# Inverting the 64x64 blocks of a delta-rule recurrence: recursion on compact 32x32 diagonal blocks instead of full-width 64x64 ones

## The reference

```
sa = einsum('bhij,bhj->bhi', s, kk_t)
s  = s * w_t[:, :, None, :] - sa[..., None] * b_t[:, :, None, :] + v_t[..., None] * k_t[:, :, None, :]
y  = einsum('bhij,bhj->bhi', s, r_t)
```

## Time and profile before

| | |
|---|---|
| median of 3 runs | 3817.77 us (3813.36 to 3818.82) |
| profiled execution | 3811.94 us, its span 3810.2 us |
| TensorE busy (matmuls) | 3230.0 us, 85% of the span |
| VectorE, ScalarE, GpSimd busy | 1983.3, 1128.4, 1046.2 us |
| the 12 passes of the recurrence | from about 2440 to 3098 us of the span |

### The profile page before, as it was taken

The page is one execution under the profiler, slowest core; times in us unless marked ns, Lnnn a source line. Parts: engine busy times, 40 slices in busy tenths (PEclk is TensorE's granted clock), DMA queues, the critical chain, the costliest instruction groups (busy, mean ns, idle before and its releaser), DMA issues. The chain is left out here.

```text
span 3810.2 us, 66276 instructions
## 1 busy us (share of the span) xinstructions
PE 3230.0 (85%) x28285; PEld 2544.4 (67%) x28285; DVE 1983.3 (52%) x2750; ACT 1128.4 (30%) x1783; POOL 1046.2 (27%) x608
## 2 busy tenths in 40 slices
PE   4989788999698879899945998599999987489896
PEld 2866476878486547687822887388888875369634
DVE  3766556880376665787022660466666633421152
ACT  2223334331322333433123221233333321322212
POOL 0321133544132213354400221243444411022100
PEclk7998899999898889999966999799999997789998
DMA  2221122333222102233334331200000021021101
GB/s 72 73 78 39 29 84 66 94 93 97 57 68 72 45 26 86 72 95 92 97 108 177 105 114 53 80 16 20 20 20 20 3 80 45 1 92 57 50 0 66
DMA packets 354104, 243.93 MB, mean 64 GB/s; under 512 B 22212, under 2 KB 330872, under 8 KB 353164
## 3 DMA queue, kind: packets, MB, share of 16 engines
q1 hardware_dynamic: 350398, 231.57, 20.3%
q10 hardware_dynamic: 3406, 8.04, 0.5%
HBM read 222.54 MB, written 17.04 MB: 63 GB/s over the span
## 5 line engine op out<-in xcount | busy, mean ns | idle before, releaser
L571 POOL TENSOR_TENSOR weights_lo<-weights_raw,weights_hi 128x1024 fp32r<-128x1024 f32 (+1 forms) x234 | 596.7, 2551 | 1227.8 <-ACT weights_hi L540 1227.8
L1139 PE MATMUL psum<-moving_hi,weights_hi 128*128 128x512 f32 x1488 | 604.2, 406 | 101.6 <-DVE weights_lo L571 53.8
L1139 PE MATMUL psum<-moving_lo,weights_hi 128*128 128x512 f32 x1488 | 590.2, 397 | 0.0
L1139 PE MATMUL psum<-moving_hi,weights_lo 128*128 128x512 f32 x1488 | 588.9, 396 | 0.0
L1139 PEld LDWEIGHTS psum<-moving_hi,weights_hi 128*128 128x128 f32 x1488 | 286.8, 193 | 184.2 <-DVE weights_lo L571 55.4
L540 ACT ACTIVATE weights_hi<-weights_raw 128x1024 fp32r<-128x1024 f32 (+2 forms) x250 | 253.9, 1019 | 291.0 <-PE psum L1139 240.3
L1139 PEld LDWEIGHTS psum<-moving_lo,weights_hi 128*128 128x128 f32 x1488 | 286.6, 193 | 61.9 <-issue 4.9
L1139 PEld LDWEIGHTS psum<-moving_hi,weights_lo 128*128 128x128 f32 x1488 | 286.1, 192 | 62.0
L1139 PE MATMUL psum<-hn_hi,even_hi 128*128 128x256 f32 (+1 forms) x480 | 162.9, 339 | 34.0 <-DVE even_lo L571 34.0
L2406 POOL TENSOR_TENSOR second_off<-second_mats,second_masks 128x256 f32<-128x256 f32 x180 | 141.3, 787 | 183.4 <-PE psum L1851 183.4
L571 POOL TENSOR_TENSOR even_lo<-even_raw,even_hi 128x1024 fp32r<-128x1024 f32 x28 | 67.5, 2409 | 361.1 <-ACT even_hi L540 361.1
(11 more groups left out here) (430 smaller groups left out, 6959.9 us busy)
## 6 DMA issues: line engine op xcount, KB each, us to landing
weights_raw<-in_w_up SPq DMA_DIRECT2D x88, 512.0 KB, 3.9
weights_raw<-in_w_in SPq DMA_DIRECT2D x78, 512.0 KB, 3.8
ada_raw<-in_ada_w SPq DMA_DIRECT2D x12, 2048.0 KB, 18.5
odd_raw<-in_od_w_in SPq DMA_DIRECT2D x16, 1024.0 KB, 5.4
even_raw<-in_ev_w_in SPq DMA_DIRECT2D x30, 512.0 KB, 3.9
weights_raw<-in_w_down SPq DMA_DIRECT2D x32, 448.0 KB, 3.7
weights_raw<-in_w_o SPq DMA_DIRECT2D x16, 512.0 KB, 4.1
weights_raw<-in_w_down SPq DMA_DIRECT2D x16, 512.0 KB, 4.1
```

The source lines that it names most:

```text
L571: ops.tensor_tensor(self.ring.lo[i % n][:, a:b], self.ring.raw[:, t % self.ring.landing, a:b], self.ring.hi[i % n][:, a:b].bitcast(F32), A ...
L1139: return nc.tensor.matmul(to, (hi, lo)[which][:, at:at + P], moving(k)[part], start=start and k == 0 and i == 0, stop=stop and k == n_k - ...
```

## The change

M, y, W and the mask `off` of the first four levels are kept *compactly*: only the two 32x32 diagonal blocks of each 64x64 matrix, one in 32 partitions, the other in the 32 below. So a chunk's matrix is 128 partitions by 32 columns, and a 64x64 product of two halves becomes four 32x32 products on the four diagonal tiles of the array, at rows and columns 0, 32, 64 and 96:

```
+def quarters_matmul(nc, out, lhsT, rhs):
+    for j in range(4):
+        ps = slice(HB * j, HB * j + HB)
+        last = nc.tensor.matmul(out[ps, :], lhsT[ps, :], rhs[ps, :], start=True, stop=True)
+    return last
+
+def halves_of_chunks(nc, out, lhsT, rhs):
+    for j in range(4):
+        hf, at = slice(64 * (j // 2), 64 * (j // 2) + 64), slice(HB * (j % 2), HB * (j % 2) + HB)
+        last = nc.tensor.matmul(out[HB * j:HB * j + HB, :], lhsT[hf, at], rhs[hf, at], start=True, stop=True)
+    return last
```

The unit "m" becomes "blocks": the diagonal blocks of M transposed and of M, both from PSUM. VectorE masks both at once into `wc` (the compact W, columns 0 to 31 transposed, 32 to 63 not), and ScalarE copies M transposed to `mt`, from which `off` is cut:

```
-                                last = halves_matmul(nc, to[:, c, :], ar[:, x, a_], bk[:, x, a_])
+                                halves_of_chunks(nc, to[:, c, 0:HB], bk[:, x, a_], ar[:, x, a_])
+                                last = halves_of_chunks(nc, to[:, c, HB:], ar[:, x, a_], bk[:, x, a_])
...
+                    pe.wait_ge(blocks_copied, GROUPS)
...
+                        elif what == "blocks":
+                            act.wait_ge(taken_dve, taken_by(n, "dve"))
+                            S.activation(mt[:, own(g), :], bank(n % BANKS, CH)[:, :, 0:HB], ACT.Identity).then_inc(blocks_copied, 1)
...
-                                made = V.tensor_tensor(buf.wb[:, slots(g), CH:], bank(n % BANKS, CH), over(pre_f + "1"), ALU.mult)
+                                made = V.tensor_tensor(wc[:, own(g), :], bank(n % BANKS, CH), over(pre_t + "1"), ALU.mult)
```

The rounds. Levels 0 to 3 (blocks 2 to 16) use `quarters_matmul`; the last level (block 32) needs one 32x32 product for y and one for W in each head and chunk, and its result isn't added but copied into its corner of `wb`:

```
                             for c in range(4):
-                                last = halves_matmul(nc, bank_y(n)[:, c, :], off[:, n % 2, c, :], buf.wb[:, slots(g).start + c, CH:])
+                                if level < last_level:
+                                    last = quarters_matmul(nc, bank_y(n)[:, c, :], off[:, n % 2, c, :], wc[:, x, HB:])
+                                else:
+                                    for hf in range(2):
+                                        last = PE.matmul(bank_y(n)[half(hf, other), c, :], buf.mats[half(hf, first), slots(g).start + c, columns_of(other)],
+                                                         wc[half(hf, first), x, HB:], start=True, stop=True)
...
                             for c in range(4):
-                                last = halves_matmul(nc, bank_w(n)[:, c, 0:CH], y_, wt)
                                 if level < last_level:
-                                    last = halves_matmul(nc, bank_w(n)[:, c, CH:], wt, y_)
+                                    quarters_matmul(nc, bank_w(n)[:, c, 0:HB], y_, wt)
+                                    last = quarters_matmul(nc, bank_w(n)[:, c, HB:], wt, y_)
+                                else:
+                                    for hf in range(2):
+                                        last = PE.matmul(bank_w(n)[half(hf, first), c, 0:HB], y_[half(hf, other), :], wt[half(hf, other), :],
+                                                         start=True, stop=True)
```

VectorE and GpSimd. The add shrinks to 128x256 elements; the last level has two copies of 32 partitions a group. GpSimd begins W with one addition of the identity where it had three operations, cuts `off` from `mt` (128x128 elements) and only for 12 rounds, and in place of the last three masks it writes the compact W into `wb` at full width (`widen`, two operations a group, zeros off the diagonal):

```
-                            n_cols = 2 * CH if level < last_level else CH
-                            w_ = buf.wb[:, slots(g), 0:n_cols]
-                            V.tensor_tensor(w_, w_, bank_w(n)[:, :, 0:n_cols], ALU.add).then_inc(w_added, 1)
+                            if level < last_level:
+                                w_ = wc[:, own(g), :]
+                                V.tensor_tensor(w_, w_, bank_w(n), ALU.add).then_inc(w_added, 1)
+                            else:
+                                dve.wait_ge(widened, 2 * g + 2)
+                                for hf in range(2):
+                                    V.tensor_copy(buf.wb[half(hf, first), slots(g), columns_of(other)], bank_w(n)[half(hf, first), :, 0:HB])\
+                                        .then_inc(last_copied, 1)
...
+                    def widen(g):
+                        pool.wait_ge(w_added, GROUPS * (last_level - 1) + g + 1)
+                        for j in range(2):
+                            G.tensor_scalar(buf.wb[:, slots(g), columns_of(j)], wc[:, own(g), 0:HB], mask("block")[:, j:j + 1], None, ALU.mult)\
+                                .then_inc(widened, 1)
```

More of the change, by code:

```diff
@@ L41 @@
 NCH = T2 // CH
+HB = CH // 2
 RET_HEADS = 8
@@ L108, in const_table @@
     t["eye64"] = s == q
-    for b in (1, 2, 4, 8, 16, 32):
+    s, q = p[:, None] % 32, np.arange(32)[None, :]
+    t["eye32"] = np.concatenate([s == q, s == q], 1)
+    for b in (1, 2, 4, 8, 16):
         off = (s // (2 * b) == q // (2 * b)) * (s // b != q // b)
-        t[f"up{b}"] = off * (s < q)
-        t[f"lo{b}"] = off * (s > q)
+        up, lo = off * (s < q), off * (s > q)
+        t[f"up{b}"] = np.concatenate([up, lo], 1) if b == 1 else up
+        t[f"lo{b}"] = np.concatenate([lo, up], 1) if b == 1 else lo
+    t["block"] = (p[:, None] // 32 % 2 == np.arange(2)[None, :]).astype(float)
     k64 = np.arange(64)
@@ L1933, in pe @@
             for c in range(4):
-                last = halves_matmul(nc, self.made(item, 2 * CH)[:, c, :], b.wb[:, s0 + c, 0:CH], b.ax[:, s0 + c, :])
+                last = halves_matmul(nc, self.made(item, 2 * CH)[:, c, :], b.wb[:, s0 + c, :], b.ax[:, s0 + c, :])
             last.then_inc(self.wau_ready, 1)
@@ L2253, in products @@
             pair_mask = "upper" if d == 0 else "lower"
-            pre_t, pre_f = ("up", "lo") if d == 0 else ("lo", "up")
+            pre_t = "up" if d == 0 else "lo"
+            first, other = (0, 1) if d == 0 else (1, 0)
+            half = lambda hf, j: slice(64 * hf + HB * j, 64 * hf + HB * j + HB)
+            columns_of = lambda j: slice(HB * j, HB * j + HB)
             over = lambda name: mask(name).unsqueeze(1).to_broadcast([P, 4, mask(name).shape[1]])
             bank = lambda b, n: psum[:, b * 512:b * 512 + 4 * n].rearrange("p (c n) -> p c n", n=n)
-            kinds = (["v"] if d == 0 else []) + ["tok", "kr", "br", "a", "m"]
+            kinds = (["v"] if d == 0 else []) + ["tok", "kr", "br", "a", "blocks"]
             units = [(g, what) for g in range(GROUPS) for what in kinds]
@@ L2270, in products @@
             BANKS = 4
-            bank_y, bank_w = lambda n: bank(n % 2, CH), lambda n: bank(2 + n % 2, 2 * CH)
-            names = "unit_ready taken_act taken_dve wt_scaled wt_begun wf_begun masked y_ready y_taken w_ready w_added "
+            bank_y, bank_w = lambda n: bank(n % 2, HB), lambda n: bank(2 + n % 2, CH)
+            names = "unit_ready taken_act taken_dve blocks_copied w_begun widened masked y_ready y_taken w_ready w_added last_copied "
             with stage(nc, names + Terms.NAMES + Recurrence.NAMES) as (block, sems):
[L2274 to L2277, removed]
+                (unit_ready, taken_act, taken_dve, blocks_copied, w_begun, widened, masked, y_ready, y_taken, w_ready,
+                 w_added, last_copied) = sems[:12]
+                terms = Terms(sems[12:12 + Terms.COUNT], i + 1, p - 1 if d == 1 and p else None)
+                rec = Recurrence(nc, sems[12 + Terms.COUNT:], i - 1, buf, psum, eye)
                 @block.sync
@@ L2293, in _ @@
                             pe.wait_ge(taken_act if by[n - BANKS] == "act" else taken_dve, taken_by(n - BANKS, by[n - BANKS]))
+                            if units[n - BANKS][1] == "blocks":
+                                pe.wait_ge(blocks_copied, units[n - BANKS][0] + 1)
                         to = bank(n % BANKS, width[what])
@@ L2422, in _ @@
                     for n in range(len(rounds) + 1):
-                        if 2 <= n < len(rounds):
+                        if 2 <= n < GROUPS * last_level:
                             off_diagonal(n)
+                        elif GROUPS * last_level <= n < len(rounds):
+                            widen(rounds[n][1])
                         for phase in terms.due(UNIT_PLACES + n, PLACES):
```

32 lines of the change are left out of this document (16 added, 16 removed).

## The result

The changed kernel takes 3998.86 us (median of 4 runs, 3998.46 to 4014.47) against 3818.3 in the same measurement (3813.36 to 3819.1). The ratio is 1.0486, with a 95% interval of 1.0459 to 1.0513: 4.9% slower, 180 us or 15 us a pass, where 1% faster was forecast. The profiled execution is the longest of the four, 4014.47 us with a span of 4012.7. The prediction was wrong in its sign, and its range (3730 to 3890) doesn't hold the result.

A forecast was written before the change was run, and what follows sets the result against it. TensorE's instruction stream was taken as the bound; 8.4 - 3.7 - 0.2 - 1.1 - 0.25 = 3.1 us a pass saved, 37 us for 12, so 3778 us, 1% faster; range 3730 to 3890.

The forecast's parts named there:

- What bounds the kernel now: Rounds, 2.10 us an iteration: TensorE's instruction stream is the bound, a product removed is time removed, until VectorE takes over.
- The products: Rounds and last level: a call of four 32x32 products takes 0.067 us for 0.117, saving 8.4 us a pass.
- a short record costs what a long one does: 32x32 products: a call stays at 0.117 us, 3872 us in all; chance 0.27 together with two of four tiles.
- two of four tiles: 32x32 products: only two tiles run at once, 0.134 us a call, 3892 us; shares the 0.27 chance.
- Changes of tile shape: Between 32x32 and 64x64 products: 0.095 us at each of 39 changes, 3.7 us a pass lost.
- "Blocks" and the start of the rounds: Units: 8 calls for 4, 0.2 us a pass; before the first round, waiting for mask and copy, 0.25 us.
- VectorE, GpSimd, ScalarE: Other engines: VectorE deciding in long phases loses 1.1 us a pass; GpSimd no cost; ScalarE none except 0.25 us at the start.
- Instructions: Instruction loading: matmuls in the rounds go from 336 to 624 a pass, 72 more in the units; no cost.
- records follow one another at 0.029 us at best: TensorE's records: a call of 8 takes 0.233 us, some 24 us a pass more, 4105 us; chance 0.06.
- The clock: TensorE: 1.2 GHz because a quarter of the array is in use instead of half; within 0.03 for anything else.

The follow-up runs named there:

- e4: Kernel before with only the first head's 64x64 products in the rounds, half the instructions in y and W: 3827.14 us, ratio 1.002.
- e1: Separate program of nothing but matmul streams, in sections by tile shape and columns; first section (four 32x32 tiles, 32 columns): packets 3.59 us apart (median).
- e3: Changed kernel with only two of the four tiles in each product of levels 0 to 3, all changes of shape kept: 3846.36 us, ratio 1.0074.
- e2: Changed kernel with 64 columns streamed instead of 32 in each 32x32 product of levels 0 to 3, same number of instructions: 3994.42 us, ratio 1.0462.
- e6: Changed kernel with VectorE transposing W, so TensorE makes one W product of four tiles for two: 3864.8 us, ratio 1.0138.

## Why the prediction was wrong, by its own steps

**What bounds the kernel now: true, but there were two bounds.** TensorE's stream was the bound, and its tiles set the pace, as e4 shows. The prediction didn't see that a second limit, the supply of instructions, stood close behind: 3.45 to 4.0 us for 256 in e1, where this kernel used 3.73.

**The products: right.** 0.067 us a call was forecast; the calls at 2861.27 to 2861.54 are 0.06 to 0.08 apart, four tiles side by side. The rivals "a short record costs what a long one does" and "two of four tiles" both fall. A tile takes a record every 34 ns here, in the first burst of e1. The prediction set beside the first rival the rule of the Trainium skill (page "TensorEngine Tiling (Array Packing)", section "Performance Considerations") that a matmul takes at least some 60 cycles. By that figure a record would need 25 ns at 2.4 GHz, an estimate, and 34 is above it: the figure isn't contradicted, but it doesn't hold a call at 0.117 either, as the prediction had taken it to.

**Changes of tile shape: right in kind, too small.** 0.095 was taken and 0.14 measured in e1. In the kernel 32 records of y and the change take 0.39 us (2840.97 to 2841.36) for 0.27 of records, and the step with its change 0.84 for 0.70: 0.12 and 0.14. Over 39 changes at 0.13 that is 1.4 us a pass more than forecast, an estimate. An iteration without a gap would be 0.39 + 0.84 + 0.61 = 1.84 us, where the prediction had 1.7 and the kernel before 2.10. With this alone put right, the sum would be 1.7 us a pass for 3.1 and the time 3798, still faster. No run shows that: e3, with the same tiles, the same changes of shape and hardly any wait for instructions, takes 3846.

**"Blocks" and the start of the rounds: too small.** By the terms for "blocks" (0.2), for the start (0.25) and for 6 changes of shape (0.57), the part of a pass up to the first y group should have grown by 1.0 us. It grew by 2.7, and by 2.5 in e3. The low clock at the start of many passes is one cause (1.2 GHz, see e3); how much is left besides wasn't separated. **VectorE, GpSimd, ScalarE: no error that matters.** The durations are above; VectorE's 1.1 us a pass disappeared because it had time in plenty.

**Instructions: this is the step that failed.** The prediction counted them rightly (1344 to 2496 in the rounds of a pass, 288 more in the units), read the packets, and then wrote "a faster stream, perhaps one packet in 2 us, still leaves the queues idle nearly all of the time. No cost". The share of time in which a queue is busy says nothing of how often it can deliver. A packet is 256 instructions and comes every 3.59 us in the first section of e1 (median, 3.36 at the least) and every 4.0 (median) in the recurrence after the change, however idle the queues are. What could be had from the profile before stood in two numbers: 144 instructions in 2.10 us are 256 in 3.73, and nowhere in that trace, in no stage, do 256 matmuls and weight loads of TensorE start in less. And the forecast iteration, 240 in 1.7, asked for 256 in 1.8, twice as many, without a row to show that it could be had. By the rule that the prediction held itself to elsewhere, the nearest row as a bound, the iteration would have been 240 x 14.6 = 3.5 us, 1.4 more than before instead of 0.4 less: 12 x 1.4 = 16.8 us a pass, 202 in all, 4014 for the profiled execution. It took 4014, the median 3999. That this comes out so well is in part luck. The 3.73 was set by the tiles (e4), so that trace couldn't tell where the supply ends, only that nothing faster had been seen; and the eleven iterations measured cost 9.6 us a pass more, with the rest of the 16 elsewhere.

The size of this term is read from e3, which has 6912 records fewer and the same shapes: 152 us of the 180 go with them. The 28 that stay, and what the shorter products should have saved besides, are left for the changes of shape, the longer start, the clock and waits for VectorE and ScalarE; these weren't separated.

The rival "records follow one another at 0.029 us at best" had this price (16.8 in the rounds) and this number, and it was put down to the array, so that "both widths keep to their columns" seemed to speak against it. That argument is about a tile. It doesn't touch a limit on the stream. With "blocks" and the shapes it came to 4105; the kernel took less, and one reason is that the units and projections leave pauses in which packets come in. Two things show that store. The 183 records of the first burst in e1 are one. The other is the beginning of the rounds, where the y groups start at 2820.58 and 2822.67, 2.09 us apart, and about 3.5 later on.

**The clock** was named as a remote way for it to go wrong, and it did fall, to 0.84 from 2440 to 3098 us, where it was 1.00. Not because of the tiles in use: e2 uses the same ones at 0.96. The cost is small beside the supply, since e2 is only 4 us shorter, within the noise, but it isn't nothing, as the starts of the passes show. What lowered it stays open.

What stays open too is what sets the two parts of the 3.6 us: the 1.1 us from the beginning of a burst to the start of the next packet, and of the 2.3 to 2.7 us from there to its first instruction the part that isn't the transfer (0.96 to 1.37 us). Whether other traffic on the queues makes them longer wasn't tried.

## What to carry to other kernels

Before splitting matmuls into smaller ones, count instructions per microsecond: a float32 matmul is four, and where a stretch already runs near 256 in 3.7 us (14 to 15 ns an instruction), expect every instruction added to cost its 14.5 ns, as it did here (e6), and no time taken out of the array to come back (e2). Read the supply from the distance between the packets of the instruction queue, not from its share, and take idle time put down to "issue" that falls in the middle of a call as its sign. A product that only makes a transpose of a block that another engine can turn is then the first to go: it brought 1% here in the kernel before, by the array's time, and 134 us in the changed one, by its instructions, where smaller tiles cost 4.9%.

## What was not expected of the hardware

- The instruction supply as above: bursts of 128 records at 10 to 13 ns each, then 1.5 to 2.4 us without any, and each packet begun 1.0 to 1.7 us after the burst before it.
- For halves, 32 moving columns are no faster than 64 (29.1 ns a record each, 58 in its tile), while 128 take 54.5, 109 in its tile. For quarters the first burst, at the high clock, has 8.5 ns a record, 34 in its tile. So it is something in the 64-wide tile other than the moving columns, perhaps its weight load, that sets the 58; this wasn't separated.
- One 32x32 tile alone held the granted clock at 0.53, mostly the 1.2 GHz level, and 51.6 ns a record. The later bursts of the first section, at the low clock, had 13.3 ns a record, 53 in each of the four tiles. A tile's pace thus depends on the clock; the supply was no faster at the higher one (packets 3.59 us apart at 0.57, 3.91 at 0.90).
- VectorE transposes 128x256 float32 elements in 32x32 blocks within SBUF in 0.445 us, hardly more than an add of the same size (0.42).
